# Attention in fixed slots: feature-major outputs, division and value split on GpSimd, and an output projection that reads them as they lie

## What is computed

```python
fox_o = fox_prompt(fq, fk, fv, flf)      # 8 heads x 64, causal, logits + cumulative log-forget bias
dsa_o = dsa_prompt(dq, iq, iw, dk, dv, ik, topk)   # 8 heads, 2 kv heads, top 256 admissible keys
mix = jnp.concatenate([fox_o, dsa_o], axis=-1) @ w_out[l]
yp = post_sublayers(yp, mix, ...)        # layer norm, SwiGLU FFN, layer norm
# each attention: p = softmax(q @ k.T * scale + bias); o = p @ v; the 32 new rows attend to 1024 past keys too
```

## Time and profile before

| what | value |
|---|---|
| median of 3 runs | 1772.08 us (1769.35 to 1781.54) |
| the profiled execution | 1774.95 us, of which the profiled span is 1773.2 us |
| PE busy | 1609.5 us, 91% of the span |
| DVE, ACT, POOL busy | 860.3, 571.1, 322.4 us |
| mean granted TensorE clock | 0.938 |

### The profile page before, as it was taken

The page is one execution under the profiler, slowest core; times in us unless marked ns, Lnnn a source line. Parts: engine busy times, 40 slices in busy tenths (PEclk is TensorE's granted clock), DMA queues, the critical chain, the costliest instruction groups (busy, mean ns, idle before and its releaser), DMA issues. The chain is left out here.

```text
span 1773.2 us, 23021 instructions
## 1 busy us (share of the span) xinstructions
PE 1609.5 (91%) x8876; PEld 1368.6 (77%) x8876; DVE 860.3 (49%) x1680; ACT 571.1 (32%) x1028; POOL 322.4 (18%) x354
## 2 busy tenths in 40 slices
PE   6999899589988598897997999999999999999985
PEld 6879899556665465655876989989989899899883
DVE  2379998956664466564556132131231321322328
ACT  3477787145553355553003101101111011111100
POOL 3423255200000000000001221212212112122116
PEclk9999999768888889798998999999999999999997
DMA  5102121020003400004102211102101111021002
GB/s 193 42 11 86 62 85 62 0 87 25 24 13 120 121 1 1 1 1 143 48 27 72 72 44 51 47 24 71 47 24 47 49 46 47 24 71 71 0 1 98
DMA packets 64750, 91.25 MB, mean 51 GB/s; under 512 B 9000, under 2 KB 51720, under 8 KB 64672
## 3 DMA queue, kind: packets, MB, share of 16 engines
q1 hardware_dynamic: 64672, 90.25, 15.4%
HBM read 77.43 MB, written 12.27 MB: 51 GB/s over the span
## 5 line engine op out<-in xcount | busy, mean ns | idle before, releaser
L1989 DVE TENSOR_TENSOR mix<-mix,down 128x512 f32<-128x512 f32 (+1 forms) x198 | 135.1, 685 | 215.2 <-PE down L1844 215.2
L1973 DVE TENSOR_TENSOR prod<-gated,up 128x1056 f32<-128x1056 f32 x22 | 27.6, 1254 | 334.7 <-PE up L1799 334.7
L1799 PE MATMUL gate<-h_hi,gu_hi 128*128 128x352 f32 x528 | 171.0, 324 | 0.6 <-POOL gu_lo L1923 0.6
L1844 PE MATMUL down<-down_hi,act_hi 128*128 128x512 f32 (+1 forms) x396 | 159.2, 402 | 12.4 <-DVE mix L1989 8.6
L1799 PE MATMUL up<-h_hi,gu_hi 128*128 128x352 f32 x528 | 170.3, 323 | 0.0
L1799 PE MATMUL gate<-h_lo,gu_hi 128*128 128x352 f32 x528 | 169.3, 321 | 0.0
L1799 PE MATMUL up<-h_lo,gu_hi 128*128 128x352 f32 x528 | 169.2, 320 | 0.0
L1799 PE MATMUL up<-h_hi,gu_lo 128*128 128x352 f32 x528 | 169.1, 320 | 0.0
L1799 PE MATMUL gate<-h_hi,gu_lo 128*128 128x352 f32 x528 | 169.1, 320 | 0.0
L1844 PE MATMUL down<-down_hi,act_lo 128*128 128x512 f32 (+1 forms) x396 | 158.3, 400 | 0.0
L1844 PE MATMUL down<-down_lo,act_hi 128*128 128x512 f32 (+1 forms) x396 | 158.2, 400 | 0.0
(11 more groups left out here) (307 smaller groups left out, 3788.6 us busy)
## 6 DMA issues: line engine op xcount, KB each, us to landing
gate_raw<-in_w_gate SPq DMA_DIRECT2D x11, 1024.0 KB, 5.2
up_raw<-in_w_up SPq DMA_DIRECT2D x11, 1024.0 KB, 5.4
down_raw<-in_w_down SPq DMA_DIRECT2D x11, 1024.0 KB, 7.4
w_raw<-in_w_in SPq DMA_DIRECT2D x9, 1024.0 KB, 5.5
x_raw<-in_xT SPq DMA_DIRECT2D x8, 528.0 KB, 8.4
key_bias<-scratch_negc SPq DMA_DIRECT2D x8, 512.0 KB, 3.6
wo_raw<-in_w_out SPq DMA_DIRECT2D x8, 512.0 KB, 4.5
x_row<-in_x SPq DMA_DIRECT2D x8, 512.0 KB, 3.5
```

The source lines that it names most:

```text
L1799: mm = nc.tensor.matmul(bank[:, ch, 0:TC], l, r, start=(k == 0 and i == 0), stop=(k == KD - 1 and i == 2))
L1844: mm = nc.tensor.matmul(pd[0:rows, i % 2, :], l, r, start=n == 0, stop=n == 5)
L1973: nc.vector.tensor_tensor(prod[:, :].rearrange("p (c r) -> p c r", c=NCH), gated[:, :].rearrange("p (c r) -> p c r", c=NCH), pu[:, :, 0:TC ...
L1989: nc.vector.tensor_tensor(o, o, pd[0:rows, i % 2, :], ALU.add).then_inc(added, 1)
```

## The change

- **Slots.** `plan` replaces `schedule`. Slot k holds: the weighted steps due (step x in slot x.k + 3, and one slot later for the first step of a batch), then the logits given to this slot, then the transposes of step k. VectorE's three outputs (batch joined, item biased, step split) share one semaphore `freed`, and TensorE waits once at the start of a slot for the largest count it needs, plus the exps at a batch's first step.
- **Logits further ahead.** Those of batches b+1 and b+2 are spread over the steps of the even batch b; odd batches have none. There are three exp areas (a, b, c) instead of two, and four places for `eT` instead of three, so `hi` no longer waits for TensorE's weighted step.
- **Feature-major outputs.** No oT and no transposes back. In the slot after a batch's last weighted step ScalarE copies the lower half of `po` (v_lo products) to its place in `mT`, VectorE adds the upper half (`joined`), and the next batch's first weighted step waits for that. In DSA both are two instructions of 256 columns on 64 partitions, in FoX one of 512.
- **Division on GpSimd.** VectorE's reciprocals `rinv` go by DMA to DRAM and come back spread over all partitions (`scales`, 256 KB); GpSimd multiplies `mT` by them (`normed`). SP waits in turn for the reciprocal, for its own store, and for the multiplication before.
- **Value split on GpSimd**, a head ahead.
- **Output projection.** mT is read as it lies: no transposes but for the 32 new rows, mT_lo on GpSimd. `rows` takes the place of `mix` for its results. Some buffers are placed elsewhere.

```diff
+def plan(batches):
+    for x in steps:
+        slots[x.k].step = x
+        x.slot = x.k + LAG + (x.part == 0)
+        slots[x.slot].weighted.append(x)
+    for batch in batches:
+        slots[batch.last.slot + 1].joined.append(batch)
+        if batch.b % 2 == 0:
+            ahead = [it for b in batches[batch.b + 1:batch.b + 3] for it in reversed(b.items)]
+            n = len(batch.parts)
+            for i in range(n):
+                slots[batch.first.k + i].logits += ahead[i * len(ahead) // n:(i + 1) * len(ahead) // n]
...
     @block.sync
-        loads(sp)
-        sp.wait_ge(out_done, len(batches))
+        for batch in batches:
+            loads(sp, batch.b)
+            if batch.sample:
+                continue
+            sp.wait_ge(recip_done, batch.b + 1)
+            sp.dma_start(c["scale_rows"][batch.b].rearrange("(q i) -> q i", i=BH), rinv[:, batch.b % 4, :])\
+                .then_inc(scales_stored, 16)
+            sp.wait_ge(scales_stored, 16 * (batch.b + 1))
+            if batch.b:
+                sp.wait_ge(normed, len(places(batch)) * batch.b)
+            sp.dma_start(scales[:, :], c["scale_rows"][batch.b].partition_broadcast(P)).then_inc(scales_loaded, 16)
...
     @block.tensor
+        for slot in slots:
+            wanted = [x.split for x in slot.weighted if not x.sample]
+            wanted += [batches[x.batch.b - 1].joined for x in slot.weighted if x.part == 0 and x.batch.b]
...
+            if max(wanted, default=0) > known:
+                known = max(wanted)
+                pe.wait_ge(freed, known)
+            for x in slot.weighted:
+                weighted(x)
+            for it in slot.logits:
...
+                logits_of(it)
+            if slot.step:
+                transposes(slot.step)
...
     @block.scalar
         def hi(x):
-            if x.copy >= LAG:
-                act.wait_ge(pv_done, x.copy - LAG + 1)
...
+        for slot in slots:
+            for batch in slot.joined:
+                if not batch.sample:
+                    act.wait_ge(pv_done, batch.last.k + 1)
+                    for out, view, _ in places(batch):
+                        last = nc.scalar.copy(out, view(po[HD:2 * HD, :]))
+                    last.then_inc(tail_done, 1)
+            if slot.step:
+                hi(slot.step)
+            for it in slot.logits:
+                exp(it)
...
+    @block.gpsimd
+            pool.wait_ge(freed, batch.joined)
+            pool.wait_ge(scales_loaded, 16 * (batch.b + 1))
+            for out, _, scale in places(batch):
...
+                nc.gpsimd.tensor_tensor(out, out, scale(scales), ALU.mult).then_inc(normed, 1)
...
     @block.vector
+        for slot in slots:
+            for batch in slot.joined:
...
+                    dve.wait_ge(tail_done, batch.b + 1)
+                    for out, view, _ in places(batch):
+                        last = nc.vector.tensor_tensor(out, view(po[0:HD, :]), out, ALU.add)
+                    last.then_inc(freed, 1)
+            for it in slot.logits:
+                biased_max(it)
+            x = slot.step
+            if x and not x.sample:
+                if x.part == 0:
...
+                    nc.vector.reciprocal(rinv[:, b % 4, :], rsum[:, b % 4, :]).then_inc(recip_done, 1)
+                dve.wait_ge(hi_done, x.k + 1)
+                nc.vector.tensor_tensor(eT_lo[s][:, cols], pt[:, x.k % TR_BANKS, cols], f32(eT_hi[s][:, cols]),
+                                        ALU.subtract).then_inc(freed, 1)
...
 def mix_out(nc, d, c):
-            transposes(0)
             for t, r0, rows in TILES:
-                if t < NT:
-                    transposes(t + 1)
                 pe.wait_ge(m_lo, t + 1)
...
+        @block.gpsimd
+            def mix_lo(t):
+                pool.wait_ge(m_hi, t + 1)
+                nc.gpsimd.tensor_tensor(mT_lo[t % 2][:, :, 0:rows], mT[:, :, r0:r0 + rows],
+                                        f32(mT_hi[t % 2][:, :, 0:rows]), ALU.subtract).then_inc(m_lo, 1)
```

More of the change, by code:

```diff
@@ L916, in schedule @@
[L916 to L954, removed]
@@ L957, in attention, with __init__ @@
-def attention(nc, ctx, pl, areas, c, tag, batches, v, v_loaded, loads, pe_first, act_first, dve_first, logits, bias,
-              sample_values, sample_cols, out_view, out_sample):
+    def __init__(self, k, batch, part):
+        self.k, self.batch, self.part = k, batch, part
+        self.sample = batch.sample
+        self.blocks = batch.parts[part]
+class Slot:
+    def __init__(self):
+        self.step, self.weighted, self.logits, self.joined = None, [], [], []
+def plan(batches):
+    steps = []
+    for batch in batches:
+        for part in range(len(batch.parts)):
+            steps.append(Step(len(steps), batch, part))
+        batch.first, batch.last = steps[-len(batch.parts)], steps[-1]
+    slots = [Slot() for _ in range(len(steps) + LAG + 2)]
+    for x in steps:
[9 more added lines that the diff above has]
+                slots[batch.first.k + i].logits += ahead[i * len(ahead) // n:(i + 1) * len(ahead) // n]
+    before = list(reversed(batches[0].items))
+    items = before + [it for slot in slots for it in slot.logits]
+    for n, it in enumerate(items):
+        it.n = n
+    did = 0
+    for it in before:
+        did += 1
+        it.biased = did
+    for slot in slots:
+        for batch in slot.joined:
+            did += 1
+            batch.joined = did
+        for it in slot.logits:
+            did += 1
+            it.biased = did
+        if slot.step and not slot.step.sample:
+            did += 1
+            slot.step.split = did
+    return steps, slots, before, items
@@ L968, in sem, with attention @@
+def attention(nc, ctx, pl, exps, scales, c, tag, batches, v, v_loaded, loads, pe_first, act_first, dve_first, logits, bias,
+              sample_values, sample_cols, places, out_sample):
     def sem(name):
@@ L971, in attention @@
     ident = c["ident"]
[L972 to L976, removed]
+    steps, slots, before, items = plan(batches)
     groups = sorted({b.group for b in batches if not b.sample})
@@ L1081, in _ @@
-        for what, x in order:
-            if what == "logits":
-                if x.sample and x.n >= 1:
-                    pe.wait_ge(biased_done, x.n)
-                elif x.n >= 2:
-                    pe.wait_ge(biased_done, x.n - 1)
-                logits(pe, x, logits_at(x)).then_inc(qk_done, 1)
-                continue
-            if x.kind != "finish":
-                transposes(x)
-            upto = x.copy - LAG + 1 if x.kind in ("block", "chunk") else x.batch.last.copy + 1
-            while done < upto:
-                weighted(copied[done])
-                done += 1
-            if x is copied[-1]:
-                while done < len(copied):
-                    weighted(copied[done])
-                    done += 1
+        for it in before:
+            if it.n >= 2:
+                pe.wait_ge(freed, items[it.n - 2].biased)
+            logits_of(it)
```

453 lines of the change are left out of this document (224 added, 229 removed).

## The result

The changed kernel takes 1845.5 us, the kernel before beside it 1774.2: ratio 1.040, 95% interval 1.036 to 1.044. It is slower, as the likeliest case had it, but by 71 us where 28 were forecast, and outside the range (1745 to 1832). Its profiled execution, the fastest of the four, has a span of 1837.2 us, 64.0 more than before; these 64 us are what the profile can account for.

What follows compares the result with a forecast made beforehand. TensorE was taken to set the pace in the attentions, not by much. Terms -14 -41 +74 +23 -5 -7.5 = +29.5 us on a 1773.2-us span gave a forecast of 1800 us, range 1745 to 1832.

Steps and rivals of the forecast that it cites:

- the likeliest case: Whole kernel: slower, 1800 us, with a range of its own of 1785 to 1818; chance 0.40.
- The clock, the step that failed: Both attentions: longer boundary waits start one 10.7-us half-clock stretch per pair of batches, 16 in all; +23 us.
- pair of stretches: FoX, kernel before: the same work takes 6.33 us at full clock and 10.71 at half, a cost of 4.38 us.
- The cap: Upper bound of the clock term: two half-clock stretches per pair of batches, capped because waits are then covered; +40 us.
- The new waits, +74: Batch boundaries: TensorE waits for the copy and join on two engines; FoX +39 us, DSA +35 us.
- Removed waits and transposes, -41 and -14: Attentions: oT, out-multiplication and late-exp waits go, -41 us; output transposes at 32 batches go, -14 us.
- Satisfied waits and the division, 0: Attentions: dropping already-met waits gains nothing (upper bound 16 us); division moved to GpSimd and SP costs 0.
- Output projection, -7.5: Output projection: transposes of eight tiles go, -6.3 us, and mT_lo(0) leaves VectorE at the start, -1.2 us.
- the lock between VectorE and GpSimd: Output projection: two-SBUF-input VectorE and SBUF-reading GpSimd instructions exclude each other; at most 2.4 us at the last tile.
- The stage ends, -5: Attention ends: FoX's 3.4-us wait for past keys goes, and about 2 us of DSA's oT wait.
- The clock collapses: Rival, attentions: two half-clock stretches per pair and upper-bound waits for FoX's even batches; about 1830 us, chance 0.12.
- around 1 us: Attention boundaries: sign of being wrong if join waits are this long, instead of about 31 waits of 1.9 to 3 us.

Runs made afterwards that it cites:

- earlier join: Changed kernel with the copy out of po and the join put one slot earlier in ScalarE's and VectorE's queues: 1776.6 us, ratio 0.999.
- the same five placed later: Changed kernel with five added matmuls per batch, placed two slots after the place of the wait: 1854.3 us, ratio 1.048.
- spread logits: Changed kernel with the logits of two batches spread over the even batch's and the following odd batch's slots, join unmoved: 1855.1 us, ratio 1.044.
- second output bank: Changed kernel with one PSUM bank moved from transposes (three to two) to outputs (one to two), no work added: 1724.4 us, ratio 0.970.

## Why the prediction was wrong, point by point

**The clock, the step that failed.** The prediction took one stretch of 10.7 us per pair of batches, 82 us more at half clock, and capped its cost at +40. The chip spent 179 us more. The price per us was about right: the 33.22-us head above costs 11.0 us more than the full-clock one, and its granted clock of 0.55 means 29.9 us at half clock, 0.37 per us; the prediction's pair of stretches has 4.4 / 10.7 = 0.41 before and (4.4 - 0.7) / 10.7 = 0.35 after the covered wait. So the term is about 66 us and not 23. A small part of that gap is a slip in the sum: it takes off 0.7 us for all 16 stretches, though its 82 additional us are only 7.7 of them; by its own price they cost 28. The part that failed is the length of a stretch in FoX. It was read off the kernel before, where full slots follow a wait, and kept. Eight stretches of 10.7 us, 86 us, were forecast for each attention; FoX had 172 us at half clock, in stretches of about 32, while DSA had 94. The runs show two handles on the time at half clock: shorter waits bring fewer or shorter stretches (two or five matmuls in the wait's place, the earlier join), and denser work behind the wait shortens them (the same five placed later). The spread logits point the same way, 134 us against 172 in spite of longer waits, but they moved VectorE's and ScalarE's work too, so how much the emptier odd batches weigh is not settled. The cap was wrong for the same reason: "twice that" still counted stretches of 10.7 us. By the Trainium skill's pricing that the prediction quotes ("TensorE: Matmul & The Clock Gate", Terms) the 179 us would cost 90, an estimate; this trace's 0.37 per us disagrees. Part of the difference is that the slower matmuls cover waits, as the next paragraph shows.

**The new waits, +74.** They were 35 us. In FoX at full clock the boundary behind an even batch waits 1.56 us or, split over two waits, 1.32 + 1.18 us, and the one behind an odd batch 1.42 us; forecast were 3.0 and 1.9. Where the clock is half the second falls to 0.59 us: slow matmuls cover it. That covering was counted as 0.7 us a stretch, against stretches a third as long. The chain itself was nearly as forecast behind an odd batch: in the timeline of all engines, ScalarE's `hi` starts at 471.20 and the weighted matmul at 473.66, 2.46 us where 2.8 were summed, 0.25 of them hand-overs (the rows show about 0.1 for those from ScalarE's copy to VectorE and on to TensorE); TensorE had 1.04 us of work beside it, not 0.9. In DSA 11 boundaries wait 18.6 us together, the longest 4.2; forecast were 35.

**Removed waits and transposes, -41 and -14.** TensorE has 192 fewer matmuls (8684 against 8876), the 128 and 64 that were named, and the oT wait is gone. But a full-clock head is no shorter for it: 22.25 us, against 445.53 - 423.96 = 21.57 in the kernel before:

```profile
423.96 0.49 PE L1074 MATMUL fox_outputs<-fox_eT_hi,fox_v_parts 128*128 128x512 f32 x1 [0.99 <-ACT fox_oT L1148]
...
445.53 0.80 PE L1074 MATMUL fox_outputs<-fox_eT_hi,fox_v_parts 128*128 128x512 f32 x1 [0.99 <-ACT fox_oT L1148]
```

The forecast's own terms for FoX make it (-21 - 7 + 39) / 8 = +1.4 a head. Without the clock the sum of the terms was nearly right (29.5 - 23 = 6.5 us forecast, 64 - 66 = -2 found), as errors in both directions met; that is luck, since the new waits alone were half of their term. That the removals are worth something where no wait replaces them shows with the second output bank: 19.60 us a head.

**Satisfied waits and the division, 0.** Right. One named claim of the change, one wait in place of several, buys nothing here. GpSimd's multiplication of 512 columns took 1.54 us where 1.2 was estimated, and nothing waited for it.

**Output projection, -7.5.** It was -3.0 and -1.7 at its start, -4.7. The transposes are gone, but TensorE still stands 5.07 us for the split of w_out, whose load is only asked for when the stage begins, and the first matmuls run at half clock:

```profile
893.14 0.77 PE L1695 MATMUL mixed<-wo_hi,mT_hi 128*128 128x512 f32 x1 [5.07 <-DVE wo_lo L1744]
```

GpSimd's subtraction took 2.87 us on the mean and not 2.4, hidden in its tile. The trace shows what lengthens it. VectorE's last addition of the layer norm (`rows`, two inputs in SBUF) takes 1.23 us in the kernel before and 2.58 on the mean now. The timeline of one tile, VectorE's two rows and GpSimd's:

```profile
928.00 1.23 DVE L1622 TENSOR_TENSOR pre<-pre,ln_gain 128x1024 f32<-128x1024 f32 x1
...
928.35 3.14 POOL L1724 TENSOR_TENSOR mT_lo<-mixT,mT_hi 128x1024 fp32r<-128x1024 f32 x1
...
929.26 3.31 DVE L1740 TENSOR_TENSOR rows<-pre,ln_shift 128x1024 f32<-128x1024 f32 x1
```

GpSimd's subtraction starts while VectorE's multiplication still runs, and takes 3.14 us; VectorE's addition starts while GpSimd's instruction still runs, and ends 1.08 us behind the end of it. Five tiles look like this. The three subtractions with no such VectorE instruction beside them take 2.34 to 2.45 us, and the two additions of full tiles with no subtraction beside them 1.23. So the lock between VectorE and GpSimd that the prediction weighs (the Trainium skill, "SBUF — State Buffer", SBUF: two separate sides) is in this trace, 2.1 us on VectorE and 0.7 on GpSimd per tile. It costs no time here, since VectorE then still stands idle for 2.5 us until the next tile's matmuls.

**The stage ends, -5.** The 3.4-us wait for the past keys is gone from the waits view, but the time between the outputs of the two attentions grew by 2.9 us. Of these, 2.2 lie between TensorE's first logits of DSA and its first outputs, where the granted clock is 0.50 against 0.65 before (643.90:681.40, and 599.20:634.50 in the kernel before).

**The rivals.** "The clock collapses" at 0.12 was the right mechanism, undersized at 1830. Its condition (waits at the upper bound, 3.4 us) was not met: in FoX the clock collapsed at waits of 1.05 to 1.7 us. Of the signs that the prediction named, the waits for the join came 26 times at 1.4 us on the mean, nearer to its "around 1 us" for being wrong than to its 1.9 to 3; GpSimd was busy 96 us more and not 60; the stretch from the end of the output projection on took 828 us in both kernels, as it said.

## What to carry to other kernels

When a timeline shows the clock falling at waits of about a microsecond, price a new order by how long TensorE then stays slow, not by its waits alone, and don't take the length of a stretch from an order that you are about to change. A few throwaway matmuls in the place of a suspected wait are a cheap test: if the time falls, it is the clock, and then it pays to look for the buffer whose single copy causes the wait. Here one PSUM bank moved from transposes to outputs, with its wait, turned a 4% loss into a 3% gain.

## What the hardware showed that was not expected

Added work in the wait's place made the kernel faster by 79 us for 160 matmuls, 0.5 us gained for each; two fifths of the dose brought most of it.

A wait's length alone did not decide whether the clock fell. One of 1.32 us in each head of the kernel with five added matmuls let it stand; one of 1.28 us with the second bank let it fall once in six times. In the changed kernel the wait of 1.42 us at 473.66 was followed by full clock, while the same wait, 1.41 us, was followed by half clock in nearly every head of the kernel with work added behind it. In the kernel before, the wait of 0.99 us at 423.96 was followed by full clock and its twin at 445.53 by half clock. Nor did it decide how long half clock lasts: 10 us or 31 to 34, by what stood around it, and with the second bank one stretch of 30.7 us stands where no wait for the join is left. What decides is open.
